# The last steps of a packed expert plan: three one-expert steps put at its end

## What is computed

```python
def moe_block(t, w_router, router_bias, w_eg, w_eu, w_ed, w_sg, w_su, w_sd):
...
    _, eidx = lax.top_k(jnp.where(emask, biased, -jnp.inf), TOP_K)
...
    hg = jnp.einsum('td,edf->tef', t, w_eg)
    hu = jnp.einsum('td,edf->tef', t, w_eu)
    a = jax.nn.silu(hg) * hu * gates.astype(t.dtype)[:, :, None]
    routed = jnp.einsum('tef,efd->td', a, w_ed)
```

## Time and profile before

| | us |
|---|---|
| median of 3 runs (1017.9 to 1020.78) | 1018.09 |
| the profiled execution | 1018.95 |
| its span in the trace | 1017.0 |
| TensorE busy in the span | 880.8 |

### The profile page before, as it was taken

The page is one execution under the profiler, slowest core; times in us unless marked ns, Lnnn a source line. Parts: engine busy times, 40 slices in busy tenths (PEclk is TensorE's granted clock), DMA queues, the critical chain, the costliest instruction groups (busy, mean ns, idle before and its releaser), DMA issues. The chain is left out here.

```text
span 1017.0 us, 13559 instructions
## 1 busy us (share of the span) xinstructions
PE 880.8 (87%) x4807; PEld 407.9 (40%) x4807; DVE 333.1 (33%) x889; ACT 175.8 (17%) x370; POOL 156.8 (15%) x130
## 2 busy tenths in 40 slices
PE   3689999989999989999999999898986988989940
PEld 0267644554554444433333333333332433434420
DVE  2634233463456532222212222222221221222228
ACT  1410011020021111211111211111111111111112
POOL 0000073000000002221112221212221221212210
PEclk9789999989999989999999999999997998989985
DMA  9987422062348779899999999999999999998946
GB/s 279 400 329 207 166 76 84 1 258 99 123 202 310 298 305 345 325 378 364 381 360 347 379 396 372 382 362 354 399 392 375 388 392 357 395 370 307 385 132 201
DMA packets 69309, 304.45 MB, mean 299 GB/s; under 512 B 9613, under 2 KB 14941, under 8 KB 44136
## 3 DMA queue, kind: packets, MB, share of 16 engines
q1 hardware_dynamic: 47578, 209.64, 53.0%
q0 software_dynamic: 13888, 37.31, 14.3%
q10 hardware_dynamic: 7776, 56.63, 13.7%
HBM read 281.69 MB, written 35.19 MB: 312 GB/s over the span
## 5 line engine op out<-in xcount | busy, mean ns | idle before, releaser
L1117 PE MATMUL bank<-arena 128*32 128x512 f32 (+2 forms) x1616 | 368.8, 629 | 24.0 <-DMA arena<-in_w_exp_up 22.6
L1117 PEld LDWEIGHTS bank<-arena 128*32 128x32 f32 (+2 forms) x1616 | 121.9, 139 | 228.0 <-issue 223.0
L1139 PE MATMUL bank<-arena 128*32 128x512 f32 (+2 forms) x808 | 174.4, 596 | 3.7 <-ACT arena L1434 3.0
L787 POOL DMA_INDIRECT moe_sums<-arena x44 | 77.1, 1751 | 401.3 <-DVE arena L1956 359.0
L1139 PEld LDWEIGHTS bank<-arena 128*32 128x32 f32 (+2 forms) x808 | 57.7, 133 | 85.0 <-issue 80.8
L1764 DVE TENSOR_TENSOR arena<-arena,bank 128x256 f32<-128x256 f32 x48 | 20.3, 422 | 189.2 <-ACT arena L1428 189.2
L1779 DVE COPY arena<-bank 128x512 f32<-128x512 f32 x48 | 33.2, 693 | 139.9 <-PE bank L1139 139.8
L870 PEld LDWEIGHTS bank<-arena 128*128 128x128 f32 (+1 forms) x440 | 56.5, 195 | 46.8 <-issue 21.9
L870 PE MATMUL bank<-arena 128*128 128x128 f32 (+1 forms) x440 | 64.6, 292 | 11.1 <-DVE arena L1559 7.1
L775 POOL DMA_INDIRECT arena<-h_rows,arena x46 | 47.6, 1036 | 150.4 <-DVE arena L1940 125.7
L890 PE MATMUL bank<-arena 128*128 128x260 f32 x256 | 61.1, 399 | 0.4 <-issue 0.4
(11 more groups left out here) (242 smaller groups left out, 552.0 us busy)
## 6 DMA issues: line engine op xcount, KB each, us to landing
arena<-in_w_exp_gate SPq DMA_DIRECT2D x64, 1024.0 KB, 12.0
arena<-in_w_exp_up SPq DMA_DIRECT2D x64, 1024.0 KB, 26.9
arena<-in_w_exp_down ACTq DMA_DIRECT2D x54, 1024.0 KB, 11.9
arena<-in_w_ada SPq DMA_DIRECT2D x12, 2048.0 KB, 10.8
arena<-in_w_exp_down SPq DMA_DIRECT2D x10, 1024.0 KB, 13.2
arena<-in_w_in SPq DMA_DIRECT2D x2, 4096.0 KB, 23.6
arena<-in_w_out SPq DMA_DIRECT2D x1, 4096.0 KB, 13.7
arena<-moe_sums SPq DMA_DIRECT2D x6, 512.0 KB, 6.2
```

What stands on the lines that cost most here:

```text
L787: pool.indirect_dma_start(out=sums, out_offset=bass.IndirectOffsetOnAxis(ap=sidx[:, par:par + 1], axis=0), in_=Y[:, (par + NT) % 2, :], in ...
L1117: ins = mm(out[c:c + m], xT[:, k, c:c + m], gu_w[q][:, :, k, :], start=(k == 0), stop=(k == KD - 1), tile_position=(0, c))
L1139: ins = mm(bank[2 + f][c:c + m, :], aT[:, par, k, c:c + m], dn_w[q][:, k, f * 512:(f + 1) * 512], start=(k == 0), stop=(k == 1), tile_posi ...
```

## The change

```diff
@@ -67,7 +67,8 @@
         else:
             steps += one_new[j]
             j += 1
-    return steps
+    alone = [[(r, 0, 4)] for r in (14, 15, 16)]
+    return [step for step in steps if step not in alone] + alone
```

## The result

The change costs 6.6 us: the ratio of the changed kernel to the one before is 1.0065, with an interval of 1.0051 to 1.0079 (20 runs each; the difference of the medians is 6.1). The medians are 1024.35 us (1020.16 to 1031.91) and 1018.22. The profiled execution took 1024.56 us, its span 1022.7, which is 5.7 over the span before. The forecast was 1027.4, in a range of 1021 to 1033.

A forecast was written before the change was run, and what follows sets the result against it. Transfers were taken to set the pace up to 907.79 us, TensorE behind it. Step 38's start at 904.5 instead of 907.8, plus a 12.6 us extra step, gave +9.3 us: 1027.4 on the 1018.09 median, range 1021 to 1033.

The forecast's parts named there:

- Step 36: First moved step, two experts: TensorE waits 1.1 us for an up projection landing at 866.4, no clock lost.
- Step 37: Second moved two-expert step: waits 7 us for weights landing at 887.0, loses clock, ends at 902.1.
- Step 38: Third moved two-expert step: waits 2.4 us for weights, loses clock, takes 15.06 us, ends at 919.6.
- Step 38's start: When its last weights land: forecast 904.5, bounds 900.8 and 907.6; before, that load landed at 907.6.
- Some of that goes to the gate loads, so I take two thirds, 3 us: 1.8 MB less competing traffic is at most 4.6 us; two thirds taken as sooner landing of step 38's weights.
- The extra step: TensorE alone has six steps to run where it had five; the added one-expert step costs 12.58 us.
- The sum: 904.5 - 907.8 + 12.6 = +9.3 us, between +4.3 (no wait or clock loss at step 38) and +12.4 (weights as late as before).
- Same: Rival: up projections keep issue order, step 38's weights land 10 us sooner, at 897.4; +2.2, 1020.3 us; chance 0.09.
- place 6: Sixth load behind rank 44's in the load list, issued after step 35; needed by step 38, before by step 39.
- the overtaking: On one queue, a gate projection issued at 860.9 landed at 868.4, ahead of an up projection issued 841.7, landed 873.4.
- Faster: Rival: waits vanish if step 38's weights are in by 893.8; 1011.4 us; chance 0.04.
- Slower still: Rival: step 39 also waits, 3 us plus lost clock, as down loads compete near 902; 1035 us; chance 0.24.

The follow-up runs named there:

- one step moved: Kernel before with only the one-expert step of rank 16 put at the end: 1023.23 us, ratio 1.0041.
- early selection: DVE loads the next selection's numbers before its down-product copy, four row-number buffers: 1018.97 us in the plan before, 1021.98 in the changed plan.
- halved loads: Gate and up loads issued after step 24 or later read half their rows: 978.0 us in the plan before, 979.26 in the changed plan.
- two steps moved: Kernel before with the one-expert steps of ranks 15 and 16 put at the end: 1022.61 us, ratio 1.0028.
- mirror plan: Kernel before with its three last two-expert steps put behind the one-expert ones: 1018.08 us, ratio 0.9985.

## Why the prediction was right, and where its sizes were off

The mechanism was right: the last pair that DMA holds up is needed one step sooner, lands less than a step sooner, and one more step stands behind it. The profile after shows each step that was named.

- **Step 36**, a wait of 1.1 us without loss of clock: 2.36 us, 3.66 us for the matmuls. **Step 37**, 7 us with loss: 6.16 us, 5.23. **Step 38**, 2.4 us with loss: 2.70 us, 5.35. None from step 39 on, as said. In all the waits for up projections are 32.2 us where I said about 29, a part of it upstream of step 36.
- **Step 38's start** was the mis-sized term. I put it at 904.5; it was 901.00. 2.1 us of the 3.5 are the earlier issue in this one execution. The rest is the step "Some of that goes to the gate loads, so I take two thirds, 3 us": the flight got 4.7 us shorter, my whole bound. The 1.8 MB that I reckoned to fall out are there (1.77), but the run with one step moved has a flight of 39.8 us without the change, so that the step priced a difference no larger than that between two executions. Bytes at the common rate were no true bound either: with half of four down loads 2.1 MB less, 5.4 us at 390 GB/s, came with a flight 12.9 us shorter than before, and 8.0 shorter than with one step moved. The load is in with the last of its pair's 32 counts, and those lie some 30 us apart, which a sum of bytes doesn't describe.
- **The extra step**, 12.58 us: the stretch from the last wait to the loop grew by 12.2, so the sum of it was right, by luck: two errors cancel. The one-expert steps 39 and 40 take 12.0 and 14.1, the second with a selection wait of 2 us that I did not see; step 38 took 14.1 in place of the 15.06 of before's step 39. With the early selection the plans are 3.9 us apart, not 6.6, a difference of 2.7 with an uncertainty of some 3; the profiles with halved loads give the selection 2.6 us (3.25 less 0.65).
- **The sum**: -6.8 + 12.2 = +5.4 in the profiles, +6.6 timed, for +9.3 forecast; both inside the bounds of +4.3 and +12.4.
- **The rivals.** *Same* fell: place 6 landed at 900.8, not at 897.4. But what I held against it, the overtaking, was a misreading of the earlier trace rows: the 868.4 of place 5's gate projection is the 16th of its pair's 32 counts, and no trace shows that load in at that time. In none of the 14 traces do the counts of a later pair of gate and up run ahead of those of the three pairs before it (at 868.3 place 3 had 29, place 5 had 16). The Trainium skill's "DMA: Bandwidth & Descriptors", section "Queues, rings and completion order", has descriptors consumed in ring order on each DMA engine; the counts fit that, though they don't tell the engines apart. So an order kept, the premise of *Same*, is not refuted; what failed is the 10 us that it was to save. *Faster* fell: place 6 was 7 us late for it. (The 390 GB/s that I held against it was no ceiling: from 860.7 to 900.8 the changed kernel's DMA moved 398.) *Slower still* fell: step 39 found place 7.

Open are the size with two steps moved, what sets the last of a pair's 32 counts, and why step 35, ahead of all edits to the plan, starts between 848.4 and 853.2 us in the profiles of kernels that agree up to there.

## What to carry to other kernels

Where a stage is bound by transfers first and by TensorE later, find the last load that is waited for: the time is its landing plus the steps behind it, so an order of steps is judged by which step needs that load, not by how many loads each step has. A step that ends sooner uses up slack elsewhere; look up the next chain (here scatter, row numbers, masks, selection) before its old length is taken as its price. And a gain ahead of a landing can be given back at the landing: in the plan of before and in the mirror plan the early selection brought new waits for weights and rows, and nothing that can be measured in the time. Last, look at what a profile's landing rests on: where two loads count on one semaphore, it can't tell the first from the second.

## What the runs showed of the hardware

- Two 1 MB loads issued 0.4 us apart on one queue, with 16 counts each on one semaphore, brought their 32 counts over some 30 us (place 5 of before: 865.4 to 898.0, the 16th at 868.3). When up was issued ahead of gate, it was the same (863.1 to 899.4, the 16th at 865.8).
- One load's flight varies between executions of the same plan: place 6's up projection took 44.7 us before and 39.8 with one step moved, which agree up to there.
- The scatter-add of 128 rows took 11.2 us from issue to landing (10.6 to 13.3 over the eight from 840 to 960 us in the changed kernel). With two buffers for its row numbers, one-expert steps 39 and 40 took 14.0 and 13.7 us with halved loads; with four, and the early selection, 12.0 and 12.1.
- A wait's length alone doesn't say whether TensorE's clock is lost. Before a step's first matmul 2.36 us cost nothing (3.66 us for 16 matmuls, granted clock 1.00 over them) and 2.70 cost 1.7 us (5.35, clock 0.68). At a selection 1.85 us was followed by 5.35 us for 16 matmuls (clock 0.68), in the mirror plan; with two steps moved, one of 3.30 us cost nothing (clock 1.00):

```profile
932.94 0.38 PE L1226 MATMUL bank<-arena 128*64 128x6 bf16 x10 [3.30 <-DVE arena L1910]
933.59 3.60 PE L1118 MATMUL bank<-arena 128*128 128x512 f32 x8
```
